# An encoder layer on one core: the left half of the first output tile before the last V products of attention

## What is computed

```python
h = rms_norm(x, norm_mix_g)
q, k, v, u = split(h @ w_in)
attn = dilated_attention_mixture(q, k, v, slopes)          # 8 heads of 64 channels
hy = hyena_operator(u, ...)                                # 512 channels
mixed = concat([rms_norm(attn, attn_out_g), rms_norm(hy, hyena_out_g)])
x = x + mixed @ w_out                                      # 1024 x 1024
x = x + expert_choice_ffn(rms_norm(x, norm_ffn_g), w_router, w_gate, w_up, w_down)
return rms_norm(x, final_g)
```

## Time and profile before

| what | value |
|---|---|
| median of 3 runs | 2149.92 us (2148.94 to 2152.68) |
| the profiled execution | 2150.25 us, of which its span 2148.4 us |
| PE busy | 2051.1 us, 95% |
| DVE busy | 1657.8 us, 77% |
| ACT busy | 1294.5 us, 60% |
| chain that ended last | 88% on PE, 6% on DVE |

### The profile page before, as it was taken

How to read it: one execution, slowest core, us unless ns; L and a number is a source line. 1 busy time by engine, 2 the same in 40 slices (tenths; PEclk the granted TensorE clock), 3 DMA queues, 4 the chain that set the end, 5 groups by cost and what they waited for, 6 DMA issues and landing times.

```text
span 2148.4 us, 27211 instructions
## 1 busy us (share of the span) xinstructions
PE 2051.1 (95%) x9878; PEld 1491.6 (69%) x9878; DVE 1657.8 (77%) x1346; ACT 1294.5 (60%) x1131; POOL 190.9 (9%) x118
## 2 busy tenths in 40 slices
PE   6999898999859999999999999999999999999996
PEld 5766667578737777777777777777777777777775
DVE  4533947573548888888888888888888888888887
ACT  4213212452247777777777777777777777777775
POOL 1000312110030101010110101011010101101000
PEclk9999999998979999999999999999999999999999
DMA  7225213404469999999999999999999999999994
GB/s 198 93 103 186 89 51 106 176 11 186 153 217 370 362 383 368 383 369 381 374 370 384 365 384 369 382 373 370 385 366 384 368 383 374 370 384 367 385 366 184
DMA packets 310264, 637.60 MB, mean 297 GB/s; under 512 B 19272, under 2 KB 83144, under 8 KB 308682
## 3 DMA queue, kind: packets, MB, share of 16 engines
q1 hardware_dynamic: 306506, 624.00, 80.0%
q0 software_dynamic: 3712, 12.98, 2.5%
HBM read 610.20 MB, written 26.74 MB: 296 GB/s over the span
## 4 chain that ended last, share of the span: by engine, by line
PE 88%; DVE 6%; issue 2%; ACT 2%; DMA 2%; POOL 0%; SPq 0%; POOLq 0%; ACTq 0%; DVEq 0%
PE bank L922 22%; PE bank L920 22%; PE bank L921 22%; PE bank L647 5%; PE bank L854 3%; PE bank L727 3%; PE bank L781 2%; PE bank L658 2%; PE bank L737 2%; PE bank L959 1%; DVE ysum_sample L1414 1%; PE bank L756 1%; PE bank L768 1%; DVE ysum_prompt L1414 1%; DVE uspec L1414 1%
## 5 line engine op out<-in xcount | busy, mean ns | idle before, releaser
L1666 DVE TENSOR_TENSOR split_ring<-breg,split_ring 128x2048 fp32r<-128x2048 f32 x525 | 1202.2, 2290 | 198.0 <-ACT split_ring L1230 198.0
L1230 ACT CAST split_ring<-breg 128x2048 fp32r<-128x2048 f32 x525 | 1004.3, 1913 | 398.7 <-PE bank L922 398.7
L920 PE MATMUL bank<-split_ring,xe_split 128*96 128x512 f32 (+1 forms) x1536 | 582.8, 379 | 1.6 <-DVE xe_split L1677 1.6
L922 PE MATMUL bank<-split_ring,xe_split 128*96 128x512 f32 (+1 forms) x1536 | 578.7, 377 | 0.0
L921 PE MATMUL bank<-split_ring,xe_split 128*96 128x512 f32 (+1 forms) x1536 | 574.7, 374 | 0.0
L922 PEld LDWEIGHTS bank<-split_ring,xe_split 128*96 128x96 f32 x1536 | 248.3, 162 | 90.4
L921 PEld LDWEIGHTS bank<-split_ring,xe_split 128*96 128x96 f32 x1536 | 249.3, 162 | 85.8
L920 PEld LDWEIGHTS bank<-split_ring,xe_split 128*96 128x96 f32 x1536 | 248.7, 162 | 85.3 <-DVE xe_split L1677 1.9
L920 PE MATMUL bank<-split_ring,ht_split 128*96 128x512 f32 x704 | 277.9, 395 | 1.7 <-DVE ht_split L1684 1.5
L922 PE MATMUL bank<-split_ring,ht_split 128*96 128x512 f32 x704 | 276.9, 393 | 0.0
L921 PE MATMUL bank<-split_ring,ht_split 128*96 128x512 f32 x704 | 276.2, 392 | 0.0
(11 more groups left out here) (217 smaller groups left out, 1699.6 us busy)
## 6 DMA issues: line engine op xcount, KB each, us to landing
breg<-in_w_down SPq DMA_DIRECT2D x176, 1024.0 KB, 7.1
breg<-in_w_up SPq DMA_DIRECT2D x175, 1024.0 KB, 7.2
breg<-in_w_gate SPq DMA_DIRECT2D x174, 1024.0 KB, 6.5
w_raw<-in_w_in SPq DMA_DIRECT2D x24, 512.0 KB, 4.2
filter_spectra<-kf_out SPq DMA_DIRECT2D x6, 1024.0 KB, 5.6
kf<-filter_spectra SPq DMA_DIRECT2D x6, 1024.0 KB, 6.9
w_out_raw<-in_w_out SPq DMA_DIRECT2D x4, 1024.0 KB, 8.9
bias<-in_attn_bias SPq DMA_DIRECT2D x8, 448.0 KB, 5.6
```

The costliest lines, as they stand in the source:

```text
L920: pe.matmul(out, x_hi, w_hi, start=start, stop=False)
L922: return pe.matmul(out, x_lo, w_hi, start=False, stop=stop)
L1230: act.copy(sp_unit[n % SPLIT_RING][0], raw[slot]).then_inc(hi_done, 1)
L1666: dve.tensor_tensor(sp_unit[s][1], raw[later_place(n, e)[0]], sp_unit[s][0].bitcast(F32), ALU.subtract).then_inc(lo_done, 1)
```

## The change

Three loops are edited; no instruction is added or dropped.

- PE: `turn_mix(0)` goes from the end of step 21 to the end of step 20. `turn_mix(1)` stays in step 23 but stands before that step's transposes of probabilities, not behind them. `project_out(0, 0)`, the left half of the first output tile, goes into step 24, behind the last transposes (units 46, 47) and ahead of the last V products. Its wait for rows of attention becomes 5 (bank 4 is free then); the right half waits for all 6.
- ACT: `mix_high(0)` and `mix_high(1)` go from steps 22 and 24 to 21 and 23.
- DVE: `mix_low(0)` goes from step 23 to 22, `mix_low(1)` from step 25 to the head of step 24, before the copies of units 46 and 47. Step 21 keeps only `norm_hyena(2)`, step 22 has no norm, `norm_attention(2)` is in step 23. `norm_attention(3)` and `norm_hyena(3)`, `(4)`, `(5)` stand behind the last row of attention.

```diff
+            for pair in range(1, PAIRS + 2):
...
+                if pair == 23:
+                    turn_mix(1)
+                if pair <= PAIRS:
+                    turn_probs(2 * pair - 2)
+                    turn_probs(2 * pair - 1)
+                if pair == 20:
+                    turn_mix(0)
+                if pair == PAIRS:
+                    project_out(0, 0)
...
-                if pair in (22, 24):
-                    mix_high((pair - 22) // 2)
+                if pair in (21, 23):
+                    mix_high((pair - 21) // 2)
...
+                if pair == PAIRS:
+                    mix_low(1)
                 if pair <= PAIRS:
                     copy_probs(2 * pair - 2)
                     copy_probs(2 * pair - 1)
...
+                if pair == 22:
+                    mix_low(0)
+                if pair == 23:
+                    norm_attention(2)
+            norm_attention(3)
+            for p in (3, 4, 5):
+                norm_hyena(p)
```

More of the change, by code:

```diff
@@ L826, in _ @@
             filter_job(len(JOBS) - 1)
-            for pair in range(1, PAIRS + 2):
-                if pair < PAIRS:
-                    scores(2 * pair)
-                    scores(2 * pair + 1)
-                if pair >= 2:
-                    times_v(2 * pair - 4)
-                    times_v(2 * pair - 3)
-                if pair <= PAIRS:
-                    turn_probs(2 * pair - 2)
-                    turn_probs(2 * pair - 1)
-                if pair in (21, 23):
-                    turn_mix((pair - 21) // 2)
             def project_out(p, half):
@@ L846, in project_out @@
                     pe.wait_ge(w_out_lo, 2 * half + 2)
-                    pe.wait_ge(attn_row, TILES)
+                    pe.wait_ge(attn_row, TILES - 1 + half)
                 if p >= 1:
@@ L883, in turn_affinities @@
                 mm.then_inc(affT_mm, 1)
+            for pair in range(1, PAIRS + 2):
+                if pair < PAIRS:
+                    scores(2 * pair)
+                    scores(2 * pair + 1)
+                if pair >= 2:
+                    times_v(2 * pair - 4)
+                    times_v(2 * pair - 3)
+                if pair == 23:
[7 more added lines that the diff above has]
+                    project_out(0, 0)
             pe.wait_ge(biased, UNITS)
@@ L887, in _ @@
             for p in range(TILES):
-                project_out(p, 0)
+                if p >= 1:
+                    project_out(p, 0)
                 if p + 2 < TILES:
@@ L1571, in _ @@
                     norm_hyena(0)
-                if pair in (20, 21, 22):
-                    norm_attention(pair - 19)
-                    norm_hyena(pair - 19)
-                if pair in (23, 25):
-                    norm_hyena(4 + (pair - 23) // 2)
-                    mix_low((pair - 23) // 2)
+                if pair == 20:
+                    norm_attention(1)
+                    norm_hyena(1)
+                if pair == 21:
+                    norm_hyena(2)
+                if pair == 22:
[5 more added lines that the diff above has]
+                norm_hyena(p)
             mean_square(N_MIX + 4, 2, W, N_FFN)
```

## The result

| | before | after |
|---|---|---|
| median of 7 runs each, taken beside each other | 2151.64 us (2148.94 to 2153.70) | 2144.65 us (2143.84 to 2147.40) |
| ratio, with its 95% interval | | 0.9968 [0.9959, 0.9978] |
| the profiled execution | 2150.25 us, span 2148.4 | 2145.64 us, span 2143.8 |

The changed kernel is faster by about 7.0 us, 0.32%. The forecast was 2142.5, its range 2140.0 to 2146.3. The two profiled executions alone are only 4.6 us apart, so not all of this gain can be read in them, and part of what follows is about that.

What follows compares the result with a forecast made beforehand. PE was taken to bound the kernel, with holes held open by DVE and a low clock; 7.9 us won at turn_xn(0) less 0.3 waiting for norm_ffn_g gave 7.6, hence 2142.5 us, range 2140.0 to 2146.3.

Steps and rivals of the forecast that it cites:

- The bound: Whole kernel: PE is busy for 95% of the span, so time PE wins ahead of the experts is won at the end.
- Tile 0's transposes at nothing: Step 21 to 20 on PE: moving them counted as nothing, with bounds of 0.7 us to either side.
- DVE up to `mix_low(0)`: DVE loses 2.65 us of norms and 1.35 of biases and copies, less 0.5 of waits; ends at about 479.9.
- DVE to `mix_low(1)`: Biases, copies, a norm, then mix_low(1) ending at 483.5; left half starts at about 483.7 after waiting about 1 us.
- The left half: First output tile on PE: 5.7 us at full clock, likeliest 1.4 more from a low stretch, ending at 490.9.
- Norms and the first residual: DVE behind the last row: bank 4 free at 498.1, PE asks at 498.35, fits with 0.2 us to spare.
- The gain: Load of norm_ffn_g into gbc: lands between 502.1 and 504.2, costing PE 0.3 us of wait on average.
- Everything behind the mark moves with it: Router, choice, gather and experts' start, behind the start of turn_xn(0) on PE, move along with it.
- given back behind the mark's chain: Rival: PE waits at turn_xn(0) or later and the clock falls; 5.1 us gained, 3.4 with two falls; group chance 0.2.
- The sum: Whole kernel: 7.9 us less 0.3 gives 7.6 us gained, so 2142.5 us for the median.
- the clock did not stay low: Rival: PE low through dense products, 4.6 us per half tile; slower beyond 2.7 halves, four give 2154.8; chance 0.04.
- That nothing would be won: Rival: DVE's queue sets when mixed tiles are ready; within 2 us of before, 2149; chance 0.14 with given back twice.

Runs made afterwards that it cites:

- e4: Kernel before in its old order, plus ten unread products on PE in each of the two holes; 2147.61 us, 0.9984 of before.
- e2: Kernel before with only the left half and mix_low(1) moved early; transposes, mix_low(0) and norms in their old steps; 2145.78 us, 0.9977 of before.
- e6: Changed kernel with the norms of tiles 1 to 5 back in their old steps; 2146.66 us, 0.9975 of before.
- e1: Changed kernel with the left half of tile 0 put back behind the last V products; 2146.29 us, 0.9974 of before.
- e8: Changed kernel run and profiled once more, with nothing altered; 2144.82 us, 0.9962 of before.
- e3: Changed kernel with norm_ffn_g loaded early into memory of its own, not into gbc behind the norms; 2144.11 us, 0.9969 of before.
- e10: Second run of the changed kernel with norm_ffn_g loaded early into memory of its own; 2140.73 us, 0.9958 of before.

## Why the prediction was right, and where by luck

The predicted times are on the clock of the execution of before, and after reached A 0.43 us later. Where a time of after is set beside a predicted one, 0.43 us of it is this shift.

- **The bound.** Right. PE's rows and its clock carried all of the difference. In e4 a change of nothing but PE's waits is seen in the timed runs.
- **Tile 0's transposes at nothing.** Nothing was waited for, as said. But I passed over what they do. The clock fell between 472 and 476 in all three profiles with the old place (before, e2, e4) and in none of the nine with the new one, though the 0.87 us of waiting ahead of it is in the rows of both kernels alike. "0.87 us of waiting was enough for the first fall" was the step that failed: it was enough in the old order only. That the eight transposes directly behind the wait are the reason is argued from the twelve profiles; they differ in other things too.
- **DVE up to `mix_low(0)`.** It ended at 479.42, predicted 479.9. The counting of norms, biases and copies held. Of the half microsecond that I left for PE's wait nothing was seen.
- **DVE to `mix_low(1)`.** Left half at 483.47, predicted 483.7; a wait of 0.97 us, predicted about 1.
- **The left half.** The likeliest case, 3 us at the low clock for 1.4 us, did not come; the bound did, 5.74 us and the right half at 491.35 (bound 491.3, likeliest 492.75). This term was mis-sized by the 1.4 us: the clock stayed at 1.00 through the half, behind a wait of 0.97 us.
- **Norms and the first residual.** In time, as counted, with no wait of PE for them at tile 1's left half.
- **The gain.** The landing, 503.3, lies in the 502.1 to 504.2 that the rows gave. The wait does not: 1.57 us and not 0.3, since PE was there at 503.36 instead of 504.6. This and the clock are one error seen twice. They cancel at the mark: 504.93 against 504.9 predicted (504.6 and 0.3), or 34.05 from A against 34.45. That this agrees so well is luck.
- **"Everything behind the mark moves with it."** Wrong in the profile. The changed kernel loses 2.9 us there in both of its profiles, by two falls of the clock. This is the rival "given back behind the mark's chain", which I gave 0.2, and its best case, PE at 503.2 and a full clock before, is the one that came; it put the price of a fall at 1.7 us, and it was 1.5. The falls came behind waits that before has as well, and not behind the one at `turn_xn(0)`. Its result for two falls, 3.4 us gained, is too small since it took the gain at the mark as 6.8 and not 8.0.
- **The sum.** 7.6 us were predicted. The profiles, one of each, show 4.6, the medians 7.0. The profiled execution of before was 1.4 us below its median of seven, that of after 1.0 above its own. The prediction took the profiled execution to lie 0.33 us above the median, by the three runs it had; the median of seven is 1.7 us higher than that of three, and most of the distance from 2142.5 to 2144.65 is this. So the timed result sits by the forecast, the profile by the rival, and what the timed runs did behind the mark is not to be seen in them. The range held the time; the reason given for the number is right up to the mark, and its last step is not.
- **The other rivals.** The mixed tile was not late; the clock did not stay low. For that one the prediction's arithmetic was off: by its own 9.3 us at full clock and 4.6 us for each slow half, the sign turns at 2.0 half tiles and not at 2.7, and four of them give 9.1 us slower and not 4.5. That nothing would be won, because DVE's queue sets when the mixed tiles are there, did not come; but DVE's order is a part of the gain, since e6 with the norms put back loses 2.7 us at the mark, and e2 moves one piece on DVE too.

## What to carry to other kernels

When an engine waits for less than a few microseconds, price the wait with the slower clock behind it: in this kernel the waits shrank by 1.9 us and the busy time by 6.1, and filling the holes with products that nobody reads won 4.6 us without closing them. Two edits that close the same hole don't add up (6.9 and 6.4 gave 8.0), so test each alone before summing, and look for a piece that both contain. And where PE is sent ahead, look for the load that does not move with it: here 0.5 MB queued behind weights took 1.6 us of the gain, and the way to the next stage ran through a store and POOL, so that 1.6 us won on PE behind the weights' issue did not arrive at the experts.

## What was unexpected of the chip

- The length of a wait did not tell whether the clock falls. It fell behind waits of 0.88 us (after, 549.55), 1.30 (e1) and 2.55 (before), not behind 0.97 (after, 483.47) nor 1.57 (after, 504.93). At two places of the program the same wait had a fall behind it in after and none in before: 0.88 (549.55) against 0.87 (557.05), and 3.12 (628.71) against 3.12 (634.86).
- One load of 0.5 MB took 3.5, 7.5 and 10.2 us from issue to landing in three places, by what was queued ahead of it.
- The two profiles of the changed kernel (after and e8) repeated these falls at the same places and agreed to 0.4 us behind the mark, and so did e3 and e10 with theirs, while the timed runs of the changed kernel spread over 3 to 4 us.
